# Delta rule: the next tile's inverse begun ahead of the last level of the present one

## The reference

```python
def step(S, inp):
    r_t, w_t, k_t, v_t, kk_t, a_t = inp
    s_kk = jnp.einsum('bhij,bhj->bhi', S, kk_t)
    S = S * w_t[:, :, None, :] - s_kk[..., None] * (kk_t * a_t)[:, :, None, :] + v_t[..., None] * k_t[:, :, None, :]
    return S, jnp.einsum('bhij,bhj->bhi', S, r_t)

_, o = lax.scan(step, s0, xs)
mean = jnp.mean(o, axis=-1, keepdims=True)
var = jnp.mean(jnp.square(o - mean), axis=-1, keepdims=True)
o = ((o - mean) * lax.rsqrt(var + GN_EPS)).reshape(bsz, t, RWKV_WIDTH) * ln_w + ln_b
bonus = (jnp.sum(rh * kh * r_k, axis=-1, keepdims=True) * vh).reshape(bsz, t, RWKV_WIDTH)
out = ((o + bonus) * g.astype(f32)).astype(pc.dtype)
```

## Time and profile before

| | us |
|---|---|
| median of 3 runs | 3549.01 (3546.9 to 3552.95) |
| the profiled execution | 3547.38 |
| its span, first instruction to last | 3545.6 |
| of it the loop of the delta rule with a state, 2391 to 2608 | 217.0 |
| TensorE busy over the span | 3219.5 (91%) |
| VectorE busy | 1712.9 (48%) |
| ScalarE busy | 1223.7 (35%) |
| GpSimd busy | 293.5 (8%) |

### The profile page before, as it was taken

One profiled execution on the slowest core, in us unless ns is written; L12 is line 12 of the kernel. 1 busy time (PEld: TensorE's weight loads), 2 busy tenths in 40 slices (PEclk: granted clock), 3 DMA queues, 4 the chain that ended last, 5 costly groups with the idle time before them and its releaser, 6 DMA issues. The chain is left out here.

```text
span 3545.6 us, 51481 instructions
## 1 busy us (share of the span) xinstructions
PE 3219.5 (91%) x20994; PEld 2821.0 (80%) x20994; DVE 1712.9 (48%) x2695; ACT 1223.7 (35%) x2257; POOL 293.5 (8%) x349
## 2 busy tenths in 40 slices
PE   5999979999698999897999988978879899999988
PEld 2999967777587999775788966667758899999877
DVE  4349716666473211265526316645555455545343
ACT  5123325656562333124534105533323111111232
POOL 1000011110010000111111110011100000000010
PEclk8999979999898999998999999989999999999999
DMA  5457550000343221234211433110012111111332
GB/s 183 158 174 230 165 199 31 22 16 7 138 155 110 79 75 61 97 118 139 101 47 37 126 99 96 38 7 2 2 67 83 54 47 42 47 47 57 109 130 95
DMA packets 200015, 309.36 MB, mean 87 GB/s; under 512 B 43000, under 2 KB 134904, under 8 KB 197772
## 3 DMA queue, kind: packets, MB, share of 16 engines
q1 hardware_dynamic: 179488, 233.59, 20.8%
q0 software_dynamic: 20336, 73.08, 6.3%
HBM read 229.80 MB, written 76.81 MB: 86 GB/s over the span
## 5 line engine op out<-in xcount | busy, mean ns | idle before, releaser
L115 PE MATMUL p_pb<-p_w_hi,h_hi 128*128 128x416 f32 (+2 forms) x1216 | 423.6, 348 | 6.8 <-DVE p_w_lo L110 6.8
L117 PE MATMUL p_pb<-p_w_hi,h_lo 128*128 128x416 f32 (+2 forms) x1216 | 421.8, 347 | 0.0
L116 PE MATMUL p_pb<-p_w_lo,h_hi 128*128 128x416 f32 (+2 forms) x1216 | 419.5, 345 | 0.0
L115 PE MATMUL fu_pf<-h_hi,fu_w_hi 128*128 128x344 f32 (+1 forms) x1056 | 339.0, 321 | 8.7 <-DVE fu_pf L3637 8.7
L116 PE MATMUL fu_pf<-h_lo,fu_w_hi 128*128 128x344 f32 (+1 forms) x1056 | 340.0, 322 | 0.0
L117 PE MATMUL fu_pf<-h_hi,fu_w_lo 128*128 128x344 f32 (+1 forms) x1056 | 338.5, 321 | 0.0
L115 PEld LDWEIGHTS p_pb<-p_w_hi,h_hi 128*128 128x128 f32 x1216 | 229.5, 189 | 8.0 <-issue 7.0
L116 PEld LDWEIGHTS p_pb<-p_w_lo,h_hi 128*128 128x128 f32 x1216 | 229.2, 188 | 2.4
L117 PEld LDWEIGHTS p_pb<-p_w_hi,h_lo 128*128 128x128 f32 x1216 | 228.9, 188 | 0.7
L115 PEld LDWEIGHTS fu_pf<-h_hi,fu_w_hi 128*128 128x128 f32 x1056 | 199.5, 189 | 9.1 <-DVE fu_pf L3637 9.1
L117 PEld LDWEIGHTS fu_pf<-h_hi,fu_w_lo 128*128 128x128 f32 x1056 | 199.5, 189 | 0.0
(11 more groups left out here) (544 smaller groups left out, 6966.7 us busy)
## 6 DMA issues: line engine op xcount, KB each, us to landing
fu_raw<-in_ffn_up SPq DMA_DIRECT2D x88, 256.0 KB, 3.1
fd_raw<-in_ffn_down SPq DMA_DIRECT2D x44, 512.0 KB, 3.5
p_slab<-in_adaln_w SPq DMA_DIRECT2D x64, 256.0 KB, 3.2
la_qkv<-p SPq DMA_DIRECT2D x16, 1024.0 KB, 5.0
p<-p_o SPq DMA_DIRECT2D x60, 208.0 KB, 2.1
s_raw<-in_w_in POOLq DMA_DIRECT2D x48, 256.0 KB, 3.7
rT<-p_stage SPq DMA_DIRECT2D x10, 896.0 KB, 5.2
p_raw<-in_ab_w_in POOLq DMA_DIRECT2D x10, 832.0 KB, 7.0
```

What stands on the lines that cost most here:

```text
L115: pe.matmul(out, left[0], right[0], start=start, stop=False)
L116: pe.matmul(out, left[0], right[1], start=False, stop=False)
L117: return pe.matmul(out, left[1], right[0], start=False, stop=stop)
```

## The change

Three helpers are called at another place. VectorE calls `begin` for tile n + 2 at the end of turn n, between `mix` and the last `grow` of tile n + 1, instead of in turn n + 1 behind `take_w` and `centre`; `begin(0)` is called ahead of the loop. TensorE calls `turn_x` ahead of `prior`, ScalarE calls `keep_x` ahead of `keep_p1`. The helpers themselves, their waits and the buffers are as before.

```diff
                 for n in range(-1, NTP):
                     i, j, chain, post = n + 1, n + 2, n >= 0, n >= 1
                     inverse, prepare = i < NTP, j < NTP
+                    if inverse:
+                        keep_x(i)
                     if chain:
                         keep_p1(n)
-                    if inverse:
-                        keep_x(i)
                     if prepare:
                         square(j)
...
                 mask(0)
+                begin(0)
                 for n in range(-1, NTP):
...
                     if inverse:
-                        begin(i)
                         grow(i, 0)
...
                     if post:
                         mix(n - 1)
+                    if prepare:
+                        begin(j)
                     if inverse:
                         grow(i, 4)
...
                     inverse, prepare = i < NTP, j < NTP
+                    if inverse:
+                        turn_x(i)
                     if chain:
                         prior(n)
                     if inverse:
-                        turn_x(i)
                         left(i, 0)
```

## The result

The changed kernel takes 3514.16 us (median of 4 runs, 3512.79 to 3517.49) against 3548.39 for the kernel before in the same runs: a ratio of 0.9903, 95% interval 0.9891 to 0.9916. It is faster by 34.2 us; the forecast was 3515, 34 us faster. The spans of the two profiled executions, 3545.6 and 3511.6, differ by 34.0.

What follows compares the result with a forecast made beforehand. Bound by a chain of hand-offs in the delta rule loop, weakest at TensorE's wait for begin; 30.4, 1.8 and 1.5 make 33.7 us off 3547.4, 3513.7, plus 1.6 for the median: 3515 us, range 3511 to 3521.

Steps and rivals of the forecast that it cites:

- the sum: Delta rule loop: 30.4 us from seven turns, 1.8 from the first with a state, 1.5 from one long half clock.
- The path from the last grow to the next first grow: Each steady delta rule turn: 4.09 us instead of 8.43, a gain of 4.34.
- one of the prediction's own signs of being wrong: Delta rule turn: the forecast is wrong if the stretch from first grow to last grows beyond 19.2 us.
- begin: VectorE, ahead of the last grow: taken as 0.80 us beside GpSimd's products, ending 0.29 behind the second, at 2471.76.
- The half clock: TensorE behind its gap: products at half clock would run at full clock, right to next grow included in the path.
- the rival: Delta rule turns: clock still falls in each, 3.06 us instead of 2.35, 5.7 in all, giving 3521; chance 0.11.
- What is late next: Steady turn: ScalarE ends last, Y at 2474.37; the centring ends half a microsecond ahead of the next grow, hidden.
- The slower rival: VectorE: begin bars the last grow until GpSimd's queue is empty, 9.7 us more in all, 3559; chance 0.03.
- the prediction's argument from that one row: TensorE, first turn with a state: clock stayed at 1.00 after a 0.88 us gap; longest gap left about 0.35.

Runs made afterwards that it cites:

- e4: Against the changed kernel: GpSimd waits behind its first level product until begin is done; 3515.8 us, ratio 0.9907 to the kernel before.
- e1: Against the changed kernel: only begin stays moved, turn_x is back behind prior and keep_x behind the copies of P1T; 3522.6 us.
- e2: Against the changed kernel: keep_x alone put back behind the copies of P1T, begin and turn_x stay moved; 3525.1 us.
- e3b: Against the kernel before: 8 unread 128x128 identity products between prior and turn_x in the seven steady turns; 3541.0 us, ratio 0.9968.
- e5: Against the changed kernel: begin waits for all six of GpSimd's level products instead of the first; 3558.5 us, ratio 1.0023 to the kernel before.
- e3: Against the kernel before: 18 unread 128x128 identity products between prior and turn_x in the seven steady turns; 3556.9 us, ratio 1.0014.

## Why the prediction was right

Its steps hold; the sum came out at 33.7 us, and 34.2 were measured. By parts, in the two profiled executions, the seven steady turns gained 32.4 us (30.4 and 1.5 in the sum) and the first turn with a state 2.0 (1.8); the turn ahead of it lost 0.2. Two small errors that partly cancel helped, and one rival's price came out by luck; both are told below.

- *The path from the last grow to the next first grow.* Predicted 4.09 us from the time at which the last grow could start; measured 3.83 from its start and 0.29 that it started late, 4.12. Summed over the eight turns the path fell from 66.0 us to 30.6, and the rest of a steady turn grew from 19.20 to 19.49 (the last of the seven has no begin and didn't grow), by the same late last grow: in e4, where it is not late, the rest is 19.19. Read by the letter this met one of the prediction's own signs of being wrong, a rest beyond 19.2; but the 0.29 is the lateness that the prediction had counted into the path, so it is not a wait of another kind. e1 and e2 show that the last 7.6 us need turn_x and keep_x both; these two without begin's move were not run.
- *begin.* Its 0.94 us lies a hair over the upper end of what the rows bounded (0.45 to 0.93), not at the 0.80 taken. That it ends 0.29 us behind GpSimd's second product was right: 0.28 in the changed kernel. What was wrong is when that product ends. The prediction reckoned two products of 0.72 from the first one's start, but the second takes 0.91, because the mixing step, with both inputs in SBUF, ran beside it. The kernel before already shows it:

```profile
2470.72 0.91 POOL L2934 TENSOR_TENSOR dr_Lm<-dr_AT,dr_levels 128x256 f32<-128x256 f32 x1
```

An end at 2471.63 instead of 2471.47 gives 0.95 us for begin by the prediction's own reckoning. In the changed kernel the second and third product, the third held up by begin:

```profile
2436.77 0.91 POOL L2934 TENSOR_TENSOR dr_Lm<-dr_AT,dr_levels 128x256 f32<-128x256 f32 x1
...
2437.64 0.91 POOL L2934 TENSOR_TENSOR dr_Lm<-dr_AT,dr_levels 128x256 f32<-128x256 f32 x1
```

The Trainium skill, "SBUF — State Buffer", section "Who interferes with whom", says that a VectorE instruction with two SBUF inputs contends with a GpSimd instruction that reads SBUF, and that what they contend for is an exclusive lock. The trace agrees that the later one waits: begin takes 0.94 us beside GpSimd and 0.41 without (e4), a product 0.91 beside the mixing step or begin and 0.73 without. But begin ends 0.28 us behind the product, less than its own 0.41, so by these records it isn't held for the whole of the product's row. It delays prior by 0.35 us instead of 0.30. There two errors partly cancel: begin ends 0.15 us later than taken, and prior's first matmul follows turn_x's by 0.41 instead of 0.50.
- *The half clock.* That the clock stays up was a step of the sum and is seen in the profile; its price, inside the sum, was not stated apart. e3b gives it: 9.0 us, where the rival took 5.7 from one turn's rows. That rival was priced too low: with 9.0 its 3521 would have been near 3524, an estimate.
- *What is late next.* As predicted it is ScalarE: Y starts 1.66 us behind prior's first matmul (predicted 1.67), and the centring is hidden.
- *The slower rival.* What kept it off is that VectorE got in behind the one product that was running and not behind the whole queue: each of the nine begins ends 0.28 us behind GpSimd's second product. Its price of 3559 agrees with e5's 3558.5 by luck. There a semaphore, not GpSimd's queue, holds begin back. The rival put 3.4 us on the lateness that e5 shows in its first turn (3.6) and 0.9 on each of seven turns, 6.3 in all; e5's eight turns with a state are only 0.8 us longer than before, and the rest is the late begin of tile 0, which the rival had left alone.

What stays open is whether e4's shorter turn makes the kernel faster; the runs spread by more than the 2.9 us in question.

## What to carry to other kernels

In a hand-written pipeline, look for a short instruction whose inputs are there early and which stands in a queue behind one that waits for the end of the present step; moved ahead of that wait it costs little (here 0.35 us of a gain of 4.3 in a turn), but its followers on the other engines (here a transpose and a copy) must move with it, or the wait only changes its name. A gap on TensorE can cost more than its length, since the products behind it may run at half clock: weigh both. And an instruction put ahead of the one on which everything waits must have its input early for certain: in e5 its lateness of 3.35 us took back the gain of nearly every turn. What bounds its length is the other engine's instruction that runs beside it, and the end of that is read from its own row, not from the mean of six merged ones.

## What the runs showed of the hardware

A product of 128x128 in float32 with the identity took 0.24 us (18 in 4.29, as two records each, in e3), at a clock of 1.00 in the steady turns, so that fillers have to be counted in time and not in number.

A VectorE instruction with both inputs in SBUF and a GpSimd product hold each other up: begin took 0.93 to 0.95 us in all nine tiles of the changed kernel and 0.41 to 0.43 in e4. The last grow, with one input in PSUM, took its usual 0.41 us beside GpSimd's third product.

A gap of 0.88 us on TensorE was followed by the full clock in the kernel before. In e3b, whose fillers are not yet in that turn, the same instructions after nearly the same gap ran at half clock:

```profile
2392.68 0.68 PE L3250 MATMUL dr_by<-ident,dr_X 64*64 64x64 f32 x16 [0.89 <-DVE dr_X L3095]
```

```profile
2394.00:2397.40 3.40, 3.40 (x64) 3.40 (x64) 0.00 (x0) 0.87 (x3) 0.00 (x0) 0.51 0.02 5
```

So the prediction's argument from that one row, that the clock stays up behind a gap of 0.88 us, doesn't hold of every execution; in the changed kernel, with 0.47 us ahead of turn_x, the clock stayed at 1.00 through the loop.

The first turn of the loop is not the same in every execution. In the changed kernel, and then in e2, the stretch at half clock and what follows it (columns as in rows 1):

```profile
2353.00:2380.30 27.30, 17.61 (x172) 14.84 (x174) 8.22 (x16) 8.80 (x18) 5.72 (x8) 0.50 0.34 4
2380.30:2390.00 9.70, 6.66 (x158) 5.50 (x155) 7.57 (x14) 4.19 (x9) 0.17 (x1) 1.00 0.01 2
```

```profile
2353.00:2393.40 40.40, 28.64 (x322) 24.24 (x322) 15.05 (x28) 12.58 (x25) 5.02 (x7) 0.50 0.21 3
2393.50:2420.00 26.50, 22.92 (x458) 19.93 (x460) 13.79 (x26) 9.62 (x22) 7.45 (x11) 1.00 0.01 2
```

With the same instructions up to there, the clock rose 27 us after 2353 in the one and 40 in the other, and the first turn (first grow to last) took 17.2 and 21.6 us. This explains 4.4 us of that one execution, more than the 3 by which e2 missed. Its other runs have no profile, but their mean granted clocks are on record: one more run had 0.955, as the profiled one, and took 3526.2 us; two had 0.958 and took 3523.5 and 3524.0. That the late clock is also behind that other run is likely, not shown.
